# A two-block transformer kernel on one core: the first weight chunk in two transfers, the memory tokens' work later, throw-away products in the first waits

## What is computed

```python
def first_block(x, mem, ...):
    h = rms_norm(x, mix_norm_g)
    proj = h @ w_in
    qa, ka, va, pb, qm = split_cols(proj, sizes)
    out_a = sliding_window_attention(rms_norm(qa), rms_norm(ka), va, attn_sinks, rel_bias)
    pb = token_shift(pb, rwkv_mu)
    out_b = rwkv7_mixer(pb, ...)
    mkv = rms_norm(mem, mem_norm_g) @ w_mem_kv
    out_m = memory_attention(rms_norm(qm), rms_norm(mk), mv)
    x = x + concat(out_a, out_b, out_m) @ w_out
    return x + conv_ffn(rms_norm(x, ffn_norm_g), ...)

def second_block(x, c, ...):
    mod = silu(c) @ w_ada + b_ada
    ...
    x = x + g2 * hierarchical_moe(h2, ...)
    return rmsnorm(x, final_g)
```

## Time and profile before

| | us |
|---|---|
| median of 3 runs | 1091.37 (1088.86 to 1094.81) |
| the profiled execution | 1096.7 |
| its span in the trace | 1094.8 |
| TensorE busy | 916.7 (84%) |
| VectorE busy | 540.0 (49%) |
| ScalarE busy | 346.5 (32%) |
| GpSimd busy | 76.4 (7%) |
| mean granted clock of TensorE | 0.936 |

### The profile page before, as it was taken

One profiled execution on the slowest core, in us unless ns is written; L12 is line 12 of the kernel. 1 busy time (PEld: TensorE's weight loads), 2 busy tenths in 40 slices (PEclk: granted clock), 3 DMA queues, 4 the chain that ended last, 5 costly groups with the idle time before them and its releaser, 6 DMA issues.

```text
span 1094.8 us, 19087 instructions
## 1 busy us (share of the span) xinstructions
PE 916.7 (84%) x8318; PEld 706.3 (65%) x8318; DVE 540.0 (49%) x1004; ACT 346.5 (32%) x678; POOL 76.4 (7%) x113
## 2 busy tenths in 40 slices
PE   5999999999999998999999988666667575667665
PEld 4686888489999887988989965333334333334332
DVE  2456588847888856798866643111212111211121
ACT  2431255236767534545553341000101000000001
POOL 3102710000000000231001000000000000000000
PEclk9999999989999999999999999888878888888888
DMA  9343472674653565786436989999999999999994
GB/s 331 133 141 133 151 269 80 231 230 154 200 185 120 222 223 211 235 246 217 133 128 231 429 325 427 429 429 429 428 430 426 430 429 429 427 429 429 429 429 184
DMA packets 76089, 316.69 MB, mean 289 GB/s; under 512 B 3983, under 2 KB 27824, under 8 KB 63456
## 3 DMA queue, kind: packets, MB, share of 16 engines
q1 hardware_dynamic: 71236, 302.24, 70.1%
q0 software_dynamic: 4624, 13.14, 4.0%
q10 hardware_dynamic: 140, 0.04, 0.0%
HBM read 312.24 MB, written 1.06 MB: 286 GB/s over the span
## 4 chain that ended last, share of the span: by engine, by line
PE 58%; DMA 27%; DVE 8%; ACT 3%; issue 2%; SPq 0%; POOL 0%; DVEq 0%; ACTq 0%
PE ps L461 56%; DMA w<-in_w_up 18%; DMA w<-in_w_gate 6%; DMA w<-in_w_down 2%; DVE sp L1812 2%; DMA w<-in_w_in 1%; DMA rot<-q 1%; PE ps L550 0%; PE ps L2625 0%; DVE acc L875 0%; ACT sp L1803 0%; ACT hts L2720 0%; ACT sd L2125 0%; PE ps L982 0%; PE ps L2057 0%
## 5 line engine op out<-in xcount | busy, mean ns | idle before, releaser
L461 PE MATMUL ps<-w,xg 128*32 128x256 f32 x2048 | 158.8, 474 | 108.0 <-DMA w<-in_w_up 84.9
L461 PE MATMUL ps<-hb,sp 128*128 128x256 f32 x1824 | 226.7, 285 | 0.0
L461 PEld LDWEIGHTS ps<-hb,sp 128*128 128x128 f32 x1824 | 220.8, 190 | 3.9 <-issue 2.8
L461 PEld LDWEIGHTS ps<-w,xg 128*32 128x32 f32 x2048 | 85.1, 131 | 180.1 <-issue 156.2
L1812 DVE TENSOR_TENSOR sp<-w,sp 128x1024 fp32r<-128x1024 f32 x122 | 144.3, 1220 | 39.6 <-ACT sp L1803 39.6
L1803 ACT ACTIVATE sp<-w 128x1024 fp32r<-128x1024 f32 x122 | 122.1, 1051 | 44.1 <-PE ps L461 44.1
L2784 DVE TENSOR_TENSOR cst<-ps,cst 64x256 f32<-64x256 f32 x32 | 13.7, 427 | 227.5 <-ACT cst L2716 227.5
L2716 ACT ACTIVATE cst<-ps 64x256 f32<-64x256 f32 x32 | 12.1, 378 | 328.1 <-PE ps L461 328.1
L2799 DVE TENSOR_TENSOR ost<-ps,cst 32x256 f32<-32x256 f32 x120 | 50.4, 420 | 100.1 <-PE ps L461 97.3
L461 PE MATMUL ps<-w,hts 128*32 128x256 f32 x1024 | 62.1, 382 | 13.9 <-ACT hts L2720 11.4
L461 PE MATMUL ps<-ht,w 128*128 128x256 f32 x256 | 62.9, 400 | 2.2 <-DMA w<-in_w_in 2.2
(11 more groups left out here) (398 smaller groups left out, 1150.9 us busy)
## 6 DMA issues: line engine op xcount, KB each, us to landing
w<-in_w_down SPq DMA_DIRECT2D x36, 2048.0 KB, 35.7
w<-in_w_gate SPq DMA_DIRECT2D x32, 2048.0 KB, 28.2
w<-in_w_up SPq DMA_DIRECT2D x32, 2048.0 KB, 32.5
w<-in_w_in SPq DMA_DIRECT2D x14, 2048.0 KB, 9.2
w<-in_w_up SPq DMA_DIRECT2D x22, 1024.0 KB, 7.7
w<-in_w_ada SPq DMA_DIRECT2D x8, 2048.0 KB, 9.1
w<-in_w_out SPq DMA_DIRECT2D x4, 2048.0 KB, 8.2
w<-in_w_ada POOLq DMA_DIRECT2D x8, 768.0 KB, 5.3
```

What stands on the lines that cost most here:

```text
L461: return q.eng.matmul(o, l, r, start=start, stop=stop, skip_group_check=True)
```

## The change

Seven things change in the opening. (1) The chunk ("in", 0) comes in two transfers of 1 MB, rows 0 to 511 under a semaphore of their own (`in_a`), rows 512 to 1023 under the buffer's; a new `first_pair_pe` waits for each half, and for the third and fourth copy of hT1, where its groups of channels need them. (2) SP issues the memory tokens behind ("in", 1) instead of ahead of it. (3) ACT copies pair 0 out ahead of the norm of the memory tokens. (4) DVE makes the first shift ahead of that norm, which is written to a buffer of its own (Mn). (5) PE turns the memory tokens behind `hsum_pe`, ahead of pair 3, and DVE copies them behind `hsum_ve`. (6) POOL's loads wait until x has landed, and its two fills come first. (7) PE gets throw-away products of 128 columns: twelve ahead of its first wait, three, three and two in the waits for the norm of x, three ahead of pair 0. Two waits of ACT on `npe` are relaxed or taken away, and the load of the final gain counts on another semaphore.

```diff
--- before.py
+++ after.py
@@ -86,7 +86,7 @@
 
 
 END = object()
-SEMS = ["par", "par1", "par2", "x_io", "mem", "cst", "cst2", "bias", "gb", "rt", "fg", "done", "go0", "go1", "go2",
+SEMS = ["par", "par1", "par2", "x_io", "in_a", "mem", "cst", "cst2", "bias", "gb", "rt", "done", "go0", "go1", "go2",
         *[f"ring{i}" for i in range(10)],
         "pc", "par_v", "nsc", "nve", "npe", "nhi", "nlo", "ht1", "ft2", "fs_v", "fs_a",
         "rp", "rp_sb", "shift", "qp", "qk_sb", "sv_sb", "bias_mm", "bias_v", "band", "lam",
@@ -202,6 +202,7 @@
 
         Xm = sb("xmem", 41264, 2048)
         Xn = sb("xn", P1 + 6288, 2048)
+        Mn = sb("mn", 50848, 2048)
         junk1 = sb("junk1", 49312, 1024)
         bs = cat[:, 768:1536]
         lt = sb("lt", 43312, 256)
@@ -377,7 +378,7 @@
 
         def ada(i):
             return ("ada", i), wcols(w_ada, 512 * i, 512)
-        for slot_no, (name, part) in [(0, (("in", 0), wcols(w_in, 1664, 512))), (1, (("in", 1), wcols(w_in, 1024, 512))),
+        for slot_no, (name, part) in [(0, (("in", 0), wcols(w_in[512:1024, :], 1664, 512, 2048))), (1, (("in", 1), wcols(w_in, 1024, 512))),
                                       (2, (("in", 2), wcols(w_in, 512, 512))), (1, (("in", 4), wcols(w_in, 1536, 128))),
                                       (0, (("in", 3), wcols(w_in, 0, 512))), (1, (("kv", 0), wcols(w_kv, 0, 512))),
                                       (2, ada(1)), (0, ada(0)), (2, ada(2)), (0, ada(3)), (1, ada(4)), (2, ada(5)),
@@ -600,6 +601,17 @@
                         free[b] = [(s["rp_sb"], n + 1)]
                     yield
 
+        def first_pair_pe(q):
+            take(q, 0)
+            w = cols8(chunks["in", 0], 512)
+            for h, tile in enumerate(PAIRS[0]):
+                for z in range(2):
+                    q.wait_ge(*((s["in_a"], 16), chunks["in", 0].tok)[z])
+                    q.wait_ge(s["ht1"], 3 + z)
+                    t = proj_pe(q, psum[0][:, 256 * h:256 * h + 256], w, R_AT[tile][1], hv, range(4 * z, 4 * z + 4))
+            t.then_inc(s["rp"], 1)
+            free[0] = [(s["rp_sb"], 1)]
+
         def rpair_pe(q, n):
             for _ in rpair_steps(q, n):
                 pass
@@ -650,7 +662,7 @@
         def qpair_sc(q, n):
             i, _, _, _, b = QPAIRS[n]
             q.wait_ge(s["qp"], QP_AT[n])
-            q.wait_ge(s["npe"], 8)
+            q.wait_ge(s["npe"], 4)
             q.wait_ge(s["par_v"], 2)
             if n > 1:
                 q.wait_ge(s["rq_mm"], n - 1)
@@ -2334,7 +2345,7 @@
             q.wait_ge(s["od_mm"], 4)
             e.dma_start(tb, A["consts"][:, CT:CW]).then_inc(s["rt"], 16)
             q.wait_ge(s["nsc"], 20)
-            e.dma_start(gf, A["final_g_2"].rearrange("(a d) -> a d", a=1).to_broadcast([128, 1024])).then_inc(s["fg"], 16)
+            e.dma_start(gf, A["final_g_2"].rearrange("(a d) -> a d", a=1).to_broadcast([128, 1024])).then_inc(s["gb"], 16)
 
         ro = [0]
 
@@ -2879,7 +2890,7 @@
                 q.wait_ge(s["f_v"], 6 * again_ + 3 * i + 1)
                 e.reciprocal(fs[:, i:i + 1], fr_[:, i:i + 1]).then_inc(s["f_v"], 1)
                 q.wait_ge(s["f_a"], 4 * again_ + 2 * i + 2)
-                q.wait_ge(s["fg"], 16)
+                q.wait_ge(s["gb"], 96)
                 q.wait_ge(s["m_cb"], 30)
                 e.scalar_tensor_tensor(out=x[:, i, :], in0=half_banks(i), scalar=fr_[:, i:i + 1], in1=gf, op0=MUL, op1=MUL).then_inc(s["f_v"], 1)
 
@@ -2891,12 +2902,14 @@
             q = Queue(e)
             e.dma_start(x, A["x"].rearrange("a (b p) d -> p (a b) d", p=128)).then_inc(s["x_io"], 16)
             e.dma_start(ident, A["consts"][:, 0:128]).then_inc(s["cst"], 16)
+            in_a, in_a_src = wcols(w_in[0:512, :], 1664, 512)
+            e.dma_start(in_a(chunks["in", 0].ap), in_a_src).then_inc(s["in_a"], 16)
             for ch in chunks.values():
                 if ch.name == ("in", 1):
                     for d, src in plist1[N_ACT:]:
                         e.dma_start(d, src).then_inc(s["par1"], 16)
+                if ch.name == ("in", 2):
                     e.dma_start(v(Xm, 2), A["mem"].rearrange("a (b p) d -> p (a b) d", p=128)).then_inc(s["mem"], 16)
-                if ch.name == ("in", 2):
                     e.dma_start(cst[:, 128:CA], A["consts"][:, 128:CA]).then_inc(s["cst2"], 16)
                     e.dma_start(cst2, A["consts"][:, CA:CT]).then_inc(s["cst2"], 16)
                 if ch.name in ADA_LATE:
@@ -2937,8 +2950,8 @@
             q.wait_ge(s["cp"], 1)
             e.activation(sml(111, 1), cpad[:, 0:1], ACT.Sqrt)
             norms_sc(q, 0, x, (s["x_io"], 16), junk1)
+            rpair_sc(q, 0)
             norms_sc(q, 1, v(Xm, 2), (s["mem"], 16), junk1)
-            rpair_sc(q, 0)
             cpad_sc(q)
             lt_sc(q)
             rpair_sc(q, 1)
@@ -3000,11 +3013,9 @@
             norms_ve(q, 0, x, Xn)
             q.wait_ge(s["par_v"], 1)
             feat_ve(q, 0, hT1, col("mix_norm_g", 0, 8), "ht1")
-            q.wait_ge(s["npe"], 4)
-            norms_ve(q, 1, v(Xm, 2), Xn)
             par_ve(q, 1, 7)
-            feat_ve(q, 1, mT, col("mem_norm_g", 0, 8), "ht1")
             shift_ve(q, 0)
+            norms_ve(q, 1, v(Xm, 2), Mn)
             shift_ve(q, 1)
             par_ve(q, 2, 5)
             par_ve(q, 3, 6)
@@ -3015,6 +3026,7 @@
             kksq_ve(q)
             kp_ve(q)
             hsum_ve(q, 0, HSB, rs, 1.0, 0.0, floor=1e-24)
+            feat_ve(q, 1, mT, col("mem_norm_g", 0, 8), "ht1")
             shift_ve(q, 3)
             kk_ve(q)
             bk_ve(q)
@@ -3072,10 +3084,11 @@
         @block.gpsimd
         def _(e):
             q = Queue(e)
+            e.memset(pzv[:, :, 0:1], 0.0).then_inc(s["r_z"], 1)
+            e.memset(Lv[:, :, :, 0:1], 0.0).then_inc(s["r_z"], 1)
+            q.wait_ge(s["x_io"], 16)
             for d, src in plist2:
                 e.dma_start(d, src).then_inc(s["par2"], 16)
-            e.memset(pzv[:, :, 0:1], 0.0).then_inc(s["r_z"], 1)
-            e.memset(Lv[:, :, :, 0:1], 0.0).then_inc(s["r_z"], 1)
             bias_gp(q)
             e.dma_start(gb[0], bc(A["b_ada_2"][:, 2048:3072], [128, 1024])).then_inc(s["gb"], 16)
             for j in range(4):
@@ -3101,15 +3114,22 @@
         @block.tensor
         def _(e):
             q = Queue(e)
+            q.wait_ge(s["cp"], 1)
+            for _ in range(12):
+                mm(q, psum[4][:, 0:128], cpad[:, 0:128], cpad[:, 0:128])
             q.wait_ge(s["cst"], 16)
             q.wait_ge(s["par"], N_GAIN)
             par_pe(q, 0, 6)
+            pace(q, 4, 3, 128)
+            q.wait_ge(s["nsc"], 1)
+            pace(q, 4, 3, 128)
+            q.wait_ge(s["nsc"], 2)
+            pace(q, 4, 2, 128)
             feat_pe(q, 0, Xn, lambda i: (s["ht1"], i + 1))
-            q.wait_ge(s["ht1"], 4)
-            rpair_pe(q, 0)
+            pace(q, 4, 3, 128)
+            first_pair_pe(q)
             q.wait_ge(s["par1"], N_PAR)
             par_pe(q, 1, 7)
-            feat_pe(q, 1, Xn, lambda i: (s["ht1"], i + 5))
             rpair_pe(q, 1)
             q.wait_ge(s["par2"], N_PAR2)
             par_pe(q, 2, 5)
@@ -3125,6 +3145,7 @@
             for _ in qpair_pe(q, 0):
                 pass
             hsum_pe(q, 0, HSB, [bsv[:, i, :] for i in range(3)], "hs", (s["r_kk"], 2))
+            feat_pe(q, 1, Mn, lambda i: (s["ht1"], i + 5))
             rpair_pe(q, 3)
             rq_pe(q, 0)
             kk_pe(q)
```

## The result

Measured side by side, the changed kernel has a median of 1101.11 us in 9 runs (1100.62 to 1113.02), the kernel before one of 1093.83 us in 9 runs (1088.86 to 1096.55). The ratio is 1.0087, with a 95% interval of 1.0064 to 1.011: slower by 7.3 us between the medians and by 9.5 us by the ratio, where I had forecast 1.2 us of gain. Two outlying runs are left out of the ratios: one of the kernel before beside experiments 5 to 8 (1227.81 us), and one of experiment 2 (1103.23 us), which comes up there.

What follows compares the result with a forecast made beforehand. The opening was taken as bound by one transfer, then TensorE's queue; 2.9 us gained at the second low-rank product less 1.75 for moved turns gives 1.2 us, from median 1091.37 to 1090.2, range 1086.0 to 1093.8.

Steps and rivals of the forecast that it cites:

- The sum without the clock: Opening up to pair 3: 2.9 us earlier at the second low-rank product, less 1.75 for moved turns, 1.2 us gained.
- the new waits ahead of the low-rank products: TensorE idles some 1.8 us ahead of the first low-rank product and 0.7 ahead of the second.
- rival B: Around 31 to 35 us: new waits cool TensorE, 1.7 us per half-clock stretch; two give 1093.6; chance 0.12.
- the fall in the earlier trace: Elsewhere in the kernel before: a stretch busy for 2.85 of 3.40 us was followed by one granted 0.50.
- The argument against B: Low-rank products: the kernel before runs them from 35.36 on without a gap, and the new waits are short.
- twelve products: Throw-away products at the start: 2.6 us from 1.2 on, ending near 3.9 under the wait for the identity; no cost.
- only moved: Memory tokens' sixteen turns, from between pair 0 and pair 1 to ahead of pair 3: 1.75 us, no gain.
- A: Opening: TensorE stays the bound if the memory tokens land by 23.3; 3.7 us gained, 1087.7; chance 0.22.

Runs made afterwards that it cites:

- experiment 5: Changed kernel with five throw-away products of 256 columns in TensorE's wait for lt: 1090.85 us, ratio 0.9968 to the kernel before.
- experiment 8: Changed kernel with one throw-away product of 256 columns in each of the nine low-rank steps: 1097.64 us, ratio 1.003 to the kernel before.
- experiment 2: Changed kernel with cpad and lt made ahead of the memory tokens' norm: 1088.40 us, ratio 0.9937; two of eight runs at 1098.71 and 1103.23.
- experiment 4: Kernel before with four idle squares on ScalarE ahead of lt, making lt late, and nothing else: 1107.78 us, ratio 1.0124.
- experiment 3: Changed kernel without all five groups of throw-away products: 1104.32 us, ratio 1.0098 to the kernel before.
- my first filling: Changed kernel with fourteen throw-away products of 256 columns in the wait for lt: 1094.37 us, ratio 1.0007 to the kernel before.
- experiment 7: Changed kernel with the memory tokens' load, norm and turns back in their old places: 1089.05 us, ratio 0.995 to the kernel before.
- experiment 6: Changed kernel with lt ahead of the memory tokens' norm and three throw-away products ahead of the low-rank stretch: 1089.05 us, ratio 0.9944.
- experiment 10: Changed kernel without throw-away products, the memory tokens' load, norm and turns in their old places: 1090.31 us, ratio 0.9976 to the kernel before.

## Why the prediction was wrong, step by step

**The sum without the clock was close to right.** Each term came out somewhat sooner than I had it, with the order of events as forecast. Pair 0 started at 12.89 (14.7): the turns took 1.97 us instead of 3.67, since the clock was up. It ended at 20.0 (22.5). ("in", 1) let pair 1 start at 21.18 (22.7). The memory tokens landed at 7.34 + 16.34 = 23.7 (25.2), lt ended at 30.64 (32.3), the first low-rank product stood at 30.70 (32.4) behind a wait that names ScalarE, and the second at 33.31 (34.8), without the wait of 0.7 that I had put there: the four records at half clock, 2.06 us, filled it. The turns cost their 1.8 us at the new place. With the clock kept up, this ends in pair 3 at 56.40 (experiment 5) and in 3.5 us of gain, where I had 1.2 (pair 3 at 57.5). Each start here is set beside a profile in which the clock rose late in pair 0, and experiment 4 shows the same code without that: some of the lead at pair 3 may be such luck. The 3.5 us come from ten runs against 34 and do not hang on it.

**The step that failed is the cost of the new waits ahead of the low-rank products.** The sum took them at their own length (1.8 and 0.7 us) and put the clock behind them at nothing; the clock stood only in rival B, with too low a price and too low a chance. B had named its place (31 to 35 us, TensorE waiting between small products), its releaser and its sign, and then priced it in stretches of 3.4 us, two of them (3.4 us lost) as the likely case and three (5.1 us) as the worst that it named. It drew on the fall in the earlier trace rows. That was not the only fall in the trace of the kernel before; I had read a longer one as well, and did not show it:

```profile
230.60:240.80 10.20, 10.20 (x50) 10.20 (x50) 5.55 (x10) 3.15 (x4) 0.14 (x2) 0.50 1.09 352
```

Behind the wait for lt stand nine thin steps and then a dense projection, and there the clock stayed down for 30.7 us, nine times 3.4: from the second low-rank product to pair 3 it took 69.57 - 33.31 = 36.3 us, against 58.73 - 37.71 = 21.0 before and 1.8 for the turns. That is some 13.4 us lost, against a lead of 4.4 at the second low-rank product; with the turns, pair 3 stands 10.8 us late.

**The argument against B was false.** I wrote that the kernel before goes through the same small products at the upper level without a gap. It does, but it enters them warm. Experiments 4 and 8 show that keeping the level and regaining it are two things: the nine steps that ran at 1.00 for 14.1 us did not come back from 0.50 in any of the four profiles with a fall and no added work (the change and experiments 2, 3 and 4), in 23 to 25 us of such steps. In all four the clock was back 3.4 to 5.6 us after the last of them, in the dense projection behind; with one product more in each step (experiment 8) it was back after 3.4. So the row that I took as evidence of safety said nothing on the case, and 0.12 was too low for a wait of over a us right ahead of a long thin stretch.

**Two smaller errors.** I counted matmul records as products (twelve products are x24 and took 4.30 us, not 2.6, still under their cover, which ended at 6.27). It made my first filling twice too long. And I took the turns' 1.75 us as "only moved"; I did not see that a faster pair 0 would have made their old place a free one, as experiment 7 shows (ratio 0.995 with the memory tokens left where they were). Moving them bought nothing that the runs can tell (0.9944 in experiment 6 against 0.995) and made the wait.

On A: the transfers were indeed early (memory tokens 23.7, ("in", 1) 21.2), yet not early enough to keep ScalarE off the path.

## What to carry to other kernels

Price a new wait of TensorE by what stands behind it, not by its length. Here waits of 0.9 to 1.6 us ahead of the dense pair 1 cost themselves, and the granted clock stayed at 1.00 behind them; waits of 0.9 to 1.4 us ahead of a long thin stretch (small products between those of another job) cost many times their length, because the clock fell and did not rise before dense work came. Where such a wait can't be removed, fill it to size with products that nobody reads, and check in the stretch table that the granted clock stays at 1.00 to the end of the thin part. And before moving work out of the way, look whether its old place is one where the engine waits anyway: the memory tokens' turns were free where they stood as soon as pair 0 was faster.

## What the runs showed of the chip

Waits of 0.9 to 1.4 us ahead of the low-rank stretch were followed by 27 to 31 us at half clock (experiments 2, 3, 4 and the change), and for 0.88 us it depended on the run, if the times of experiment 2 are read rightly. I had not expected a fall after so short a wait, nor that a fall could last so long in a stretch that reads as 100% busy. A fall is not shown to need such a wait: every profile, the kernel before included, has a stretch of 0.50 of 6.8 to 10.2 us somewhere between 224 and 260 us, and many have one of 3.4 us near 65 to 80 or 190 to 206; their cause was not tried. Nor is the kernel before quite safe: of its 34 runs beside experiments 5 to 8, three took 1098.38, 1101.49 and 1103.57 us, each with a mean granted clock of 0.928 against 0.934 to 0.941 in the others. They have no profile.

The Trainium skill, "TensorE: Matmul & The Clock Gate", Part 4, says that turns do not count as activity for the clock. In experiment 10 nothing but sixteen turns, 3.56 us of them, ran on TensorE between 10.04 and 13.74, and pair 0 behind them ran at the upper level from its first product (7.14 us for the pair). Experiment 4 agrees: 3.68 us of turns and a wait of 1.72 us, and the upper level from pair 0's first product. The measurement decides: here the clock rose with turns alone. In the kernel before, whose code is the same up to there, 3.67 us of turns did not raise it, so it differs from run to run.
